# A hybrid attention and recurrence block: raw weight tiles, one residual load and some head products are placed later in their queues

## The reference, cut to what matters

```python
h = rmsnorm(x, w_norm_pre)                    # x: 2048 x 1024
q_a, k_a, v_a, z_a, q_r, f_r, i_r, z_r = split(h @ w_in)
o_a = sliding_window_sink_attention(rope(q_a), rope(k_a), v_a, sinks) * silu(z_a)
o_r = hgrn2_chunkwise(q_r, f_r, i_r, lb)      # gated recurrence, 4 heads, chunks of 64
o_r = rmsnorm(o_r, hgrn_norm) * silu(z_r)
y = concat([o_a, o_r]) @ w_out
x = x + rmsnorm(y, w_norm_post)
```

## Time and profile before

| | |
|---|---|
| median of three runs | 883.18 us |
| the profiled execution, its own time | 880.8 us |
| its span, first to last instruction | 879.0 us |
| PE busy | 855.7 us, 97% |
| DVE, ACT, POOL busy | 635.3, 520.4, 114.6 us |
| mean granted TensorE clock | 0.997 |
| moved by DMA | 211.2 MB, 240 GB/s over the span |

### The profile page before, as it was taken

One profiled execution on the slowest core, in us unless ns is written; L12 is line 12 of the kernel. 1 busy time (PEld: TensorE's weight loads), 2 busy tenths in 40 slices (PEclk: granted clock), 3 DMA queues, 4 the chain that ended last, 5 costly groups with the idle time before them and its releaser, 6 DMA issues.

```text
span 879.0 us, 12449 instructions
## 1 busy us (share of the span) xinstructions
PE 855.7 (97%) x4430; PEld 701.4 (80%) x4430; DVE 635.3 (72%) x1125; ACT 520.4 (59%) x1033; POOL 114.6 (13%) x84
## 2 busy tenths in 40 slices
PE   7999999999998999999999999999998999999997
PEld 6887888888786778888888878887886887888785
DVE  6878868763665899767346789887775367988846
ACT  7766456673574558567246555865842755676544
POOL 0000013520200000433020000144300000004210
PEclk9999999999999999999999999999999999999999
DMA  8685755649967954453779684454799574444496
GB/s 317 233 312 197 282 201 178 230 144 389 413 220 268 399 223 163 172 198 114 260 282 339 221 358 174 147 178 173 254 381 369 193 286 144 144 144 164 165 324 258
DMA packets 59981, 211.20 MB, mean 240 GB/s; under 512 B 6672, under 2 KB 6928, under 8 KB 59920
## 3 DMA queue, kind: packets, MB, share of 16 engines
q1 hardware_dynamic: 57184, 203.46, 63.2%
q10 hardware_dynamic: 2736, 6.95, 2.0%
HBM read 157.95 MB, written 52.43 MB: 239 GB/s over the span
## 4 chain that ended last, share of the span: by engine, by line
PE 64%; DVE 16%; ACT 8%; DMA 6%; issue 4%; SPq 1%; POOL 0%; DVEq 0%; ACTq 0%
PE bank L569 44%; DMA kept_lo<-w_lo 3%; PE bank L825 2%; PE bank L578 2%; PE turn_b L825 2%; PE score_b L825 2%; DVE kv_tok L1356 2%; DMA w_lo<-kept_lo 2%; PE score_b L602 2%; PE turn_b L626 1%; PE turn_b L578 1%; PE score_b L578 1%; DVE q_gate L1449 1%; PE turn_b L679 1%; PE bank L670 1%
## 5 line engine op out<-in xcount | busy, mean ns | idle before, releaser
L569 PE MATMUL bank<-h_hi,w_hi 128*128 128x512 f32 x832 | 325.4, 392 | 8.7 <-DMA w_lo<-kept_lo 7.7
L569 PE MATMUL bank<-h_hi,w_lo 128*128 128x512 f32 x832 | 327.4, 394 | 0.0
L569 PE MATMUL bank<-h_lo,w_hi 128*128 128x512 f32 x832 | 326.2, 392 | 0.0
L569 PEld LDWEIGHTS bank<-h_hi,w_hi 128*128 128x128 f32 x832 | 156.6, 188 | 42.4 <-DMA w_lo<-kept_lo 9.0
L569 PEld LDWEIGHTS bank<-h_lo,w_hi 128*128 128x128 f32 x832 | 156.4, 188 | 34.8 <-issue 3.3
L569 PEld LDWEIGHTS bank<-h_hi,w_lo 128*128 128x128 f32 x832 | 156.4, 188 | 32.9 <-issue 0.2
L1681 POOL TENSOR_TENSOR mix_lo<-v_r,mix_hi 128x512 fp32r<-128x512 f32 x16 | 21.1, 1322 | 550.0 <-ACT v_r L1113 550.0
L1234 DVE TENSOR_TENSOR w_lo<-w_raw,w_hi 128x1024 fp32r<-128x1024 f32 x37 | 45.9, 1248 | 33.6 <-ACT w_hi L899 33.1
L1356 DVE STREAM_TRANSPOSE kv_tok<-k_mid 32x128 f32<-32x128 f32 x192 | 58.1, 302 | 2.8
L899 ACT ACTIVATE w_hi<-w_raw 128x1024 fp32r<-128x1024 f32 x38 | 39.8, 1051 | 22.9 <-issue 10.3
L914 ACT ACTIVATE g_a<-g_a 128x512 f32<-128x512 f32 x32 | 20.3, 633 | 40.3 <-DVE g_a L1314 40.3
(11 more groups left out here) (265 smaller groups left out, 1551.4 us busy)
## 6 DMA issues: line engine op xcount, KB each, us to landing
w_hi<-kept_hi SPq DMA_DIRECT2D x108, 512.0 KB, 3.8
w_lo<-kept_lo SPq DMA_DIRECT2D x108, 512.0 KB, 4.7
w_raw<-in_weights SPq DMA_DIRECT2D x46, 512.0 KB, 5.8
kept_hi<-w_hi SPq DMA_DIRECT2D x34, 512.0 KB, 6.3
kept_lo<-w_lo SPq DMA_DIRECT2D x34, 512.0 KB, 7.2
x_in<-in_x_rows SPq DMA_DIRECT2D x8, 1024.0 KB, 7.7
x_in<-in_x SPq DMA_DIRECT2D x15, 512.0 KB, 7.3
out<-q_gate ACTq DMA_DIRECT2D x9, 512.0 KB, 8.4
```

The costliest lines, as they stand in the source:

```text
L569: mm = pe.matmul(acc(w)[:, :], stationary[:, s, k, :], moving[:, k, :], start=(m == 0), stop=(m == 3 * KT - 1), skip_group_check=True)
```

## The change

It moves these things.

- `save_split` of the last three raw tiles (i = 37 to 39) all stand ahead of the load of tile 1, step 7; before, one stood ahead of each of the loads of steps 7, 8 and 9.
- `load_sums` from step 6 to step 8, `save_sums` from step 12 to 13, `sum_weights` and `sums_high` one step later.
- Tile 2's residual from step 39 of tile 2 to step 1 of tile 3, both halves.
- Tile 2's output stores from ACT's queue to SP's, at step 3 of tile 3 behind that step's load.
- In DVE's `out_fast` the low part of the sum of squares comes before the wait for the residual.
- In tiles 2 and 3 `head_scores` of heads 2 and 3 (and with them `head_out` of heads 1 and 2) go from product 12 to 15 and from 16 to 20 of their step, `head_states` of heads 2 and 3 from 16 to 18 and to 20, `head_sum` of head 2 from 16 to 20.

```diff
-SUMS_IN, SUMS_OUT = 6, 12
-SUMS_AT = 5
-RES_AT = ((WT - 3, WT - 1),) * FAST + ((P3B, P3B),) * (TILES - FAST - 1) + ((H0, H0 + 1),)
+SUMS_IN, SUMS_OUT = 8, 13
+SUMS_AT = 6
+RES_AT = ((WT - 3, WT - 1),) * FAST + ((None, None),) * (TILES - FAST - 1) + ((H0, H0 + 1),)
...
+            def store_y(t, stores):
+
+                for b, cols, pieces in stores:
+                    sp.wait_ge(finished.sem, finished.after(t, pieces - 1))
+                    sp.dma_start(out[bass.ds(t * N + b * P, P), cols[0] * N:(cols[-1] + 1) * N].rearrange("p (h n) -> p h n", n=N),
+                                 q_gate[:, 2 * b + cols[0]:2 * b + cols[-1] + 1, :]).then_inc(stored[b // 2], 16)
...
-                    if LATE + RAW_SLOTS <= i < FRESH + RAW_SLOTS:
+                    if LATE + RAW_SLOTS <= i <= FRESH:
                         save_split(i - RAW_SLOTS)
+                    if i == FRESH + 1:
+                        for late in range(FRESH + 1 - RAW_SLOTS, FRESH):
+                            save_split(late)
                     if i >= FRESH:
                         load_split(t, w)
...
+                    if w == 1 and t > FAST:
+                        load_residual(t - 1, 0)
+                        load_residual(t - 1, 1)
+                    if w == RAW_SLOTS - 1 and t > FAST:
+                        store_y(t - 1, STORES)
...
-                return gate(h), (14, 20, 12, 16)[h] if t else (14, 16, 18, 18)[h]
+                return gate(h), (14, 20, 15, 20)[h] if t >= FAST else (14, 20, 12, 16)[h] if t else (14, 16, 18, 18)[h]
...
-                    if h and w == gate(h) + 1 and m == (20 if t >= DVE_TURN and h == 1 else 16):
+                    if h and w == gate(h) + 1 and m == ((0, 20, 18, 20)[h] if t >= FAST else 20 if t >= DVE_TURN and h == 1 else 16):
                         head_states(t, h)
-                    if w == out_step(h) + 1 and m == (20 if t >= DVE_TURN and h == 0 else 16 if h < HEADS - 1 else 18):
+                    if w == out_step(h) + 1 and m == ((20, 16, 20, 18)[h] if t >= FAST else 20 if t >= DVE_TURN and h == 0 else 16 if h < HEADS - 1 else 18):
                         head_sum(t, h)
...
-                    for b, cols, pieces, pool_pieces in STORES if t >= FAST else PLAIN_STORES:
+                    for b, cols, pieces, pool_pieces in PLAIN_STORES if t < FAST else ():
...
-                for i in range(2) if t + 1 < TILES else ():
-                    post_last(t, i)
+                if t + 1 < TILES:
+                    for i in range(2):
+                        post_last(t, i)
+                    dve.wait_ge(x_high, t + 1)
+                    dve.tensor_tensor(mix_lo[:, 0, :], x_acc[:, :], mix_hi[:, 0, :], ALU.subtract).then_inc(x_low, 1)
                 dve.wait_ge(res_loaded, t * 32 + 32)
...
-                if t + 1 < TILES:
-                    dve.wait_ge(x_high, t + 1)
-                    dve.tensor_tensor(mix_lo[:, 0, :], x_acc[:, :], mix_hi[:, 0, :], ALU.subtract).then_inc(x_low, 1)
```

More of the change, by code:

```diff
@@ L105 @@
 V_PLACE = tuple(range(V_TILE + 1, V_TILE + 5))
-STORES = ((2, (0, 1), 2, 0), (3, (0,), 3, 0), (3, (1,), 4, 0), (0, (0, 1), 6, 0), (1, (0, 1), 8, 0))
-LAST_STORES = STORES[:-1] + ((1, (0,), 7, 0), (1, (1,), 8, 0))
+STORES = ((2, (0, 1), 2), (3, (0,), 3), (3, (1,), 4), (0, (0, 1), 6), (1, (0, 1), 8))
+LAST_STORES = STORES[:-1] + ((1, (0,), 7), (1, (1,), 8))
 PLAIN_STORES = ((0, (0, 1), 1, 1), (1, (0, 1), 3, 0), (2, (0, 1), 4, 2), (3, (0,), 5, 0), (3, (1,), 6, 0))
-SUMS_IN, SUMS_OUT = 6, 12
-SUMS_AT = 5
-RES_AT = ((WT - 3, WT - 1),) * FAST + ((P3B, P3B),) * (TILES - FAST - 1) + ((H0, H0 + 1),)
+SUMS_IN, SUMS_OUT = 8, 13
+SUMS_AT = 6
+RES_AT = ((WT - 3, WT - 1),) * FAST + ((None, None),) * (TILES - FAST - 1) + ((H0, H0 + 1),)
 def forget(h):
@@ L531, in _ @@
                         load_residual(t, 1)
[L532 to L538, removed]
+            store_y(TILES - 1, LAST_STORES)
             sp.wait_ge(stored[0], 32 * TILES + 48)
```

## The result

The changed kernel takes 886.7 us (median of eight runs, 885.66 to 889.5) against 883.08 of the kernel before beside it: ratio 1.0039, interval 1.0025 to 1.0053, so 2.2 to 4.7 us slower. Forecast was 887.5. Its profiled execution has a span of 885.0 us against 879.0.

| us | before | after | difference |
|---|---|---|---|
| tile 1's first product | 226.44 | 226.95 | +0.5 |
| from there to the first `weigh` of tile 1 | 70.20 | 74.17 | +4.0 |
| from there to tile 2's first product | 150.94 | 150.83 | -0.1 |
| from there to the first `weigh` of tile 2 | 62.87 | 69.72 | +6.9 |
| from there to tile 3's first product | 152.85 | 148.34 | -4.5 |

What follows compares the result with a forecast made beforehand. PE, busy 97% of the span, was taken as the bound, with DVE close behind. Terms 1.7 + 6.1 - 0.9 - 0.9 - 3.4 + 1.7 = +4.3 on 883.2 gave 887.5 us, range 881 to 891.5.

Steps and rivals of the forecast that it cites:

- Direction and mechanism: Tiles 1 and 2: late raw tiles stop DVE at part 0, so PE waits at `turn` and `weigh`; slower, chance 0.60.
- The wait of 5 to 7 us: DVE's part 0 in tiles 1 and 2: a wait of 5 to 7 us for the raw tiles.
- The chain of 30.95 us: Tiles 1 and 2: from the raw tiles' landing at DVE's part 0 to PE's first `weigh`, 30.95 us.
- Tile 1's raw tiles: Tile 1: raw tiles land at 267.4, 1.27 us per half, `weigh` at 298.4; 1.7 us lost.
- The clock: Tiles 1 and 2: of two pairs of PE waits, one causes a fall to 1.2 GHz; 1.7 us lost.
- 6.1 forecast: Tile 2: raw tiles behind step 8's load land at 485.6, `weigh` at 516.6 against 510.45; 6.1 us lost.
- The split into 2.5: Tile 2's loss: 2.5 us from part 3's new place, 3.6 us from waiting for the raw tiles.
- The heads: Heads of tiles 2 and 3: four products come ahead of the last DVE release; 0.9 us won in each.
- The rival that all waits go: Heads: PE paces, all 3.9 us of waits go, no clock fall; +0.5 in all, 883.7; chance 0.12.
- From tile 2 to 3: Tile 3's start: without the residual ahead, step 0's load lands at 658.2, not 663.3; 3.4 us won.
- the cover there: Tile 3's start: time between `finish_y` ending about 670.5 and DVE's next work at 673; 2.5 us.
- Rival 3: Tile 3: SP's stores hold its loads if `finish_y` ends after 677; at 680, 3 us more, 890.5; chance 0.06.

Runs made afterwards that it cites:

- step 9's load held: The changed kernel with the load of step 9 in tiles 1 and 2 issued only when all four raw tiles are in; 886.97 us, ratio 1.0042.
- three saves ahead: Kernel with sums back in both tiles, but tile 1's raw tiles loaded behind all three saves, ahead of step 7's load; 876.61 us, ratio 0.9924.
- the late load alone: Kernel with sums back in both tiles, but tile 2's raw tiles loaded behind step 8's load, parts still from step 5; 883.01 us, ratio 0.9987.
- the heads alone: The kernel before with only the moved `head_scores`, `head_states` and `head_sum`; 881.54 us, ratio 0.9983.
- part 3 one step later: Kernel with sums back in both tiles, but tile 2's four sum parts start at DVE's step 6, raw tiles loaded early; 876.43 us, ratio 0.9921.

## Why the prediction was right, point by point

**Direction and mechanism: right.** Raw tiles later in the queue, DVE waiting at part 0, PE at `turn` and `weigh`: the two kernels with the sums put back in one tile show it for each. The wait of 5 to 7 us named for part 0 came in tile 2 (6.81); in tile 1 it was 9.49, and `scores` waited too, which was not forecast. The kernel with the sums back in both takes 12.8 us off the changed kernel's 886.7 (873.91; against its own before, 1.1% faster instead of 0.4% slower).

**The chain of 30.95 us: right.** It is 30.62 to 30.64 wherever DVE waited for the raw tiles with all four parts from step 6 on: both tiles of the changed kernel and of the one with step 9's load held, tile 1 or 2 of those with one tile put back (302.76 - 272.13, 515.95 - 485.33), and tile 1 with three saves ahead. It could be read from gaps of another tile because DVE there doesn't wait for PE: in the changed kernel it stands idle for 4.3 us between part 0 and `weigh` in each tile, every time for ACT, which waits for DVE.

**Tile 1's raw tiles: mis-sized.** Landing at 267.4 was forecast, with 270.0 as the outer bound; part 0 started at 270.50, half a microsecond past it. Of the 3.1 us, 1.5 are the load of step 6, in at 251.1 instead of 249.6: its second half took 6.0 us to land instead of the page's median of 4.7, with the saves behind it already moving (see the last section); the 14 halves behind it took about 19.4 us, 1.38 each, instead of 1.27. The term was +1.7 with a clock fall of +1.7 beside it; the trace has +4.0 to `weigh`.

**The clock: wrong, and it made up for that.** One fall was counted at 1.7 us. It fell twice, and cost nothing: both falls lie around `turn` and before `weigh`, where PE waited anyway. `weigh` is 30.62 behind part 0 at each of them, and also in tile 2 of the kernel with tile 1's raw tiles back, where the clock was at 0.98 again from 512 to 516 and PE waited 1.76 us at `weigh` instead of 0.57. The step that failed is "one fall where PE paces": after waits caused by a late DVE, PE doesn't pace. If the fall is counted with tile 1, the two errors together gave that tile +3.4 against +3.9; that they cancel is luck. The row that the forecast took for "1.00 after 3.35 us alone" ends 0.7 us behind that wait; the stretch behind it, 664 to 668, bears it out:

```profile
664.00:668.00 4.00, 4.00 (x20) 3.29 (x19) 3.30 (x6) 0.00 (x0) 0.00 (x0) 1.00 1.02 374
```

**Tile 2: 6.1 forecast, 6.9 measured.** The raw tiles were there 11.3 us after the load of step 8 was issued, against 10.2. The split into 2.5 for part 3's place and 3.6 for the wait holds for the first number (2.2 to `weigh` with the load early) but not as two losses that add up: the late load alone costs 9.0, and the step later takes part of that back.

**The heads: right.** 0.9 each was forecast; 1.0 in tile 2 and 0.6 in tile 3 with the heads alone. The rival that all waits go is refuted: 0.41, 0.81 and 0.55 us stay, and the last is still for DVE's `a_t`.

**From tile 2 to 3: right.** 3.4 forecast, 3.5 measured (4.5 less 1.0 for the heads). The times of the forecast count from PE at 659.95, and tile 3 began at 670.01, so they are compared from tile 3's first product. `finish_y` started 6.5 us behind it where 5 was forecast and ended 11.9 behind it where 10.5 was; DVE's next work came 13.0 behind it, as forecast, so the cover there was 1.1 us instead of 2.5. The load of step 4 went out 12.3 us behind it where 11 was forecast. PE shows no wait there, so both covers held, more narrowly than written. Rival 3's trigger, `finish_y` ending at 677, is 17 behind the first product and was not met.

**The sum.** +4.3 on the profiled execution was forecast (885.1); it took 886.8. The median of 886.7 is nearer to 887.5 than the terms deserve, and that is in part luck: the traces differ by 6.0, the medians by 3.6, and the 2.4 us between the profiled execution and the median were carried over as they were, and the trace after lies on its median. Two sums of the prediction don't add up as written, and nothing hung on them: the open time is 13.3 us, not 14, and 255.4 + 4.7 + 3 x 1.27 is 263.9, not 264.8.

## What to carry to other kernels

When an engine's work up to a consumer doesn't wait for that consumer, find the one wait at the head of its queue and measure from there: the start of part 0 plus a fixed chain gave the start of `weigh` to 0.02 us in seven places, while the loss of a single moved step depended on what else was late. Moving a transfer behind urgent ones helps only if its own consumer can wait; here saves together, residual and stores late and head products later are worth 1.1% once the raw tiles stay early. Size a transfer in a crowded queue from rows of a crowded queue: for the load of step 6 the median over the whole kernel was 1.3 us too short.

## What the runs showed of the hardware

In these traces a fall of the granted clock cost time only where PE paces. In the changed kernel two falls cost nothing, with 0.50 and 0.51 over 4 us; in the kernel with three saves ahead the fall reached past `weigh` and took 2.7 us, in the one with part 3 one step later 1.6. And a wait of about 3 us doesn't decide whether it falls: behind 3.29 us in tile 1 it was 0.57, behind 3.21 us at the same place 1.00; behind 3.27 us at tile 3 it was 0.68, behind 3.35 us in the kernel before 1.00, from 664 to 668. What decides it, these runs don't show.

What is issued behind a transfer can delay it, though SP issues its DMAs in one order. The second half of the load of step 6 in tile 1 landed 4.5 or 4.6 us after its issue in the seven traces where nothing was issued behind it for 3.4 us or more, and 5.9 to 6.1 us after it in the seven where a save followed 0.5 us behind; what is ahead of it is the same in all. The view of the tile `w_lo`, before and then after:

```profile
L452 SPq DMA_DIRECT2D w_lo<-kept_lo x1: 433/433/433, 244.9 to 244.9; - x1
...
DMA to landing us min/median/max: 4.6/4.6/4.6
...
L452 SPq DMA_DIRECT2D w_lo<-kept_lo x1: 433/433/433, 245.1 to 245.1; - x1
...
DMA to landing us min/median/max: 6.0/6.0/6.0
```
